# Attention with v stationary: p*v for two heads on column halves, probabilities scaled before the product, three parts summed in PSUM

## The chip, the cores and the metric

The kernel runs on one core of one Trainium2 chip. The metric is device time in microseconds (us), the median over repeated executions. One execution was also recorded by the profiler; its rows are the ones shown here. TensorE is the matrix engine, VectorE (DVE), ScalarE (ACT) and GpSimd (POOL) work beside it, and SyncE issues the weight loads.

## The reference, cut to what matters

Three transformer blocks run one after the other on 512 tokens of width 1024. The first has an attention of 8 heads over 512 keys with a multiplicity bias (called b1 here), a memory attention of 4 heads over 256 keys (mem), and a convolution branch with a layer norm. The two that follow (layers 0 and 1 of the second block, "layers" below) each have a causal attention with a forget gate (fox, 8 heads), and an attention (nsa, 8 query heads, 2 key heads) whose output is a gated sum of three parts:

```python
p_s = softmax(where(valid_s, s, -inf)); o_s = einsum('bgrqk,bgqkd->bgrqd', p_s, vg)   # selected: sel
p_w = softmax(where(valid_w, s, -inf)); o_w = einsum('bgrqk,bgkd->bgrqd', p_w, vwin)  # window: win
p_c = softmax(where(valid_c, s, NEG_BIG)) * valid_c; o_c = einsum('bgrqn,bgnd->bgrqd', p_c, vc)
o_n = g[..., 0:1] * o_c + g[..., 1:2] * o_s + g[..., 2:3] * o_w
```

With 512 tokens, 8 blocks of 64 and 16 to be selected, every block is selected, and the window of 512 covers all keys, so sel and win are both plain causal attentions. o_c has 31 compressed keys.

## The kernel before, in words

Each engine has a program written out by hand; semaphores order them. Weights stream from memory in blocks of 128x1024 through a ring of three slots; POOL splits each block into a high and a low part (L372, L375), and `linear` (L406) does three matmuls per 128x128 chunk (L422 to L424), the third with the low part. A split of block b waits until TensorE is done with block b-3. After a tile, an engine takes the PSUM bank (`took`), and the next tile on that bank waits for that.

The attentions run in *units*: one head, one tile of 128 queries. Units come in pairs of heads that sit on the two row halves (partitions 0 to 63 and 64 to 127) of the q and k tiles. Block 1 has 32 b1 units of 512 keys, then 16 mem units of 256. A layer has 32 fox units, then 32 sel, then 32 win units; their rows have 128 keys times (query tile + 1), in the order of tiles 0, 2, 1, 3.

`attend` is one loop per engine over the unit index i, with stages that lag:

- TensorE (L506): q*k of units i and i+1 in every second step (L533), with the gate rows and causal masks of the layers added to the bank (L540, L541); the transposes of p of unit i-2 (L547); p*v of unit i-4 with the transposed p stationary and the 64 columns of v moving (L567). Then what fills the step: `between1` (layer norm over the convolution and transposes of outputs, in block 1), `compressed` (the attention on 31 keys, during fox), or, during sel and win, two of the eight chunks of a gate tile (six matmuls), all gate tiles on bank 3. After the loop come transposes of the outputs (`turn_out`).
- ScalarE (L865): tanh of a gate tile, copy of the transposed p (L880), exp with its row sum (L887).
- VectorE (L1227): first, every fourth unit, the gate tile off bank 3 (L1234); then the row minimum of the new pair (L1243 for b1, L1246 otherwise), one convolution tap (L1177), `compressed`, and for unit i-4 the reciprocal of the sum (L1257), for sel and win the product with the gate (L1260), and the scaling of the output into `o1`, `oa` or `on` (L1265, L1271).

At the end of a layer's attention the outputs `oa` and `on` are transposed (L503), copied (L921) and split (L1277) for the output projection (`mix`). In block 1 `o1` goes the same way (L607, L646).

```python
mm = nc.tensor.matmul(ps[6 + j % 2][:, 0:HD], pT[:, j % 3, c * P:(c + 1) * P], v_,
                      start=c == 0, stop=c == n - 1)
...
if c0 == 0:
    if bank in last_on_bank:
        pe.wait_ge(*took(last_on_bank[bank]))
```

Of the kernel before, what the change touches and what calls it, by code (L numbers as in the profile page):

```python
# [17 lines left out]
P = 128  # L18
S = 512
D = 1024  # L20
DC = D // P
# [22 lines left out]
IN1_TAPS = {5: 4, 8: 3, 11: 3, 14: 3, 17: 5, 18: 3, 19: 5, 20: 3, 21: 4}  # L44
# [22 lines left out]
def build(nc, xT, memT, positions, wstream, params, fconst, bconst, lncount, trig2, out):  # L67
# [4 lines left out]
    with ctx:  # L72
# [26 lines left out]
        lnr = at("lnr", [S], f32, T + 12 * KIB)  # L99
        lni = at("lni", [S], f32, T + 14 * KIB)  # L100
# [5 lines left out]
        o1 = at("o1", [TT, 768], f32, R + 51 * KIB)  # L106
        lnc = at("lnc", [TT, S], f32, R + 67 * KIB)
        srow = at("srow", [2, S], f32, R + 75 * KIB)
# [19 lines left out]
        vsw = at("vsw", [2, TT, P], f32, R + 48 * KIB)  # L128
        kc = at("kc", [2, NCMP], f32, R + 52 * KIB)
        vbd = at("vbd", [2, 256], f32, R + 52 * KIB + 512)  # L130
        hidc = at("hidc", [2, 2, 62], f32, R + 54 * KIB + 512)
        gates = at("gates", [TT, 24], f32, R + 55 * KIB + 512)
        c3 = at("c3", [S], bf16, R + 56 * KIB)
        lf = at("lf", [TT, 8], f32, R + 57 * KIB)
        fgs = at("fgs", [S], f32, R + 57 * KIB + 128)
        z32 = at("z32", [3, TT, 32], f32, R + 59 * KIB + 256)
        s8 = at("s8", [5, TT, 8], f32, R + 60 * KIB + 896)
        oa = at("oa", [TT, 512], f32, R + 66 * KIB)
        on = at("on", [TT, 512], f32, R + 74 * KIB)
# [6 lines left out]
        ya_hi = at("ya_hi", [4, S], f32r, R + 32 * KIB)  # L146
        ya_lo = at("ya_lo", [4, S], f32r, R + 40 * KIB)
        yn_hi = at("yn_hi", [4, S], f32r, R + 48 * KIB)
        yn_lo = at("yn_lo", [4, S], f32r, R + 56 * KIB)
        mt = at("mt", [2, S], f32, R + 74 * KIB)  # L150
# [10 lines left out]
        prow = at("prow", [3, S], f32, T)  # L161
        pT = at("pT", [3, S], f32, T + 6 * KIB)
        crow = at("crow", [256], f32, T + 12 * KIB)
        cprob = at("cprob", [8, 32], f32, T + 13 * KIB)
        cprobT = at("cprobT", [256], f32, T + 14 * KIB)
# [23 lines left out]
        def pcol(name, i=0, n=1):  # L189
# [25 lines left out]
        scored, row_min, row_exp, p_turned, p_kept, pv_done, o_kept = (  # L215
            sem(n) for n in ("scored", "row_min", "row_exp", "p_turned", "p_kept", "pv_done", "o_kept"))
        conv_taps, ln_sum, ln_centred, ln_sq, ln_rt, ln_full, ln_hi, ln_lo = (
            sem(n) for n in ("conv_taps", "ln_sum", "ln_centred", "ln_sq", "ln_rt", "ln_full", "ln_hi", "ln_lo"))
        o_turned, o_hi, o_lo = sem("o_turned"), sem("o_hi"), sem("o_lo")
# [7 lines left out]
        c_scored, c_shift, c_exp, c_prob, c_turned, c_kept, c_pv, c_o = (  # L227
            sem(n) for n in ("c_scored", "c_shift", "c_exp", "c_prob", "c_turned", "c_kept", "c_pv", "c_o"))
# [82 lines left out]
        UN = [(k, p + 4 * r, t) for k in ("sel", "win") for p in range(4) for t in T_ORDER for r in range(2)]  # L311
# [12 lines left out]
        def turn_bank(u1, c):  # L324

            return (u1 + c) % 3 if c < 3 else c

        LN_AT, TURN_AT = 33, (38, 40, 42, 44)
        LIN_OF = {FIRST["fox", l]: l for l in range(LAYERS)}
# [36 lines left out]
        def _(pool):  # L366
# [16 lines left out]
            for b0, b1 in RUNS:  # L383
# [3 lines left out]
                for b in range(b0 + (b1 - b0) // RING * RING, b1):  # L387
                    split(b % RING, b // RING + 1, b)
                if b1 < NBLOCKS:
# [13 lines left out]
        def _(pe):  # L403
# [96 lines left out]
            def turn_out(src, bank):  # L500

                for t in range(TT):
                    mm = nc.tensor.transpose(ps[bank][:, t * P:(t + 1) * P], src[:, t, :], ident)  # L503
                mm.then_inc(o_turned, 1)

            def attend(u0, u1, gates_from=None, gate_tiles=()):  # L506

                for i in range(u0, u1 + 4):
                    if i < u1 and (i - u0) % 2 == 0:
                        kind, w = units[i][0], width(i)
                        plain = kind in ("b1", "mem")
                        if units[i] == ("mem", 0, 0):
                            pe.wait_ge(qk_final, len(QK))
                        for u in (i, i + 1):
# [11 lines left out]
                            if u - u0 < 3 and gates_from is not None:  # L529
                                pe.wait_ge(*took(last_on_bank[u % 3]))  # L530
                            if u - u0 >= 3:
                                pe.wait_ge(row_min if units[u - 3][0] == "b1" else row_exp, u - 2)
                            mm = nc.tensor.matmul(ps[u % 3][:, 0:w], q_, k_, start=True, stop=plain)  # L533
                            if plain:
                                mm.then_inc(scored, 1)
                        for u in () if plain else (i, i + 1):
                            _, h, t = units[u][:3]
                            bank = ps[u % 3]
                            if kind == "fox":
                                nc.tensor.matmul(bank[:, 0:w], headsel[0:96, h, :], c3[0:96, 0:w], start=False, stop=False)  # L540
                            nc.tensor.matmul(bank[:, t * P:w], identb, causal, start=False, stop=True).then_inc(scored, 1)  # L541
                    j = i - 2
                    if u0 <= j < u1:

                        pe.wait_ge(row_exp, j + 1)
# [1200 lines left out]
```

## Time and profile before

| | before |
|---|---|
| median of 3 runs | 2360.43 us (2360.38 to 2363.29) |
| profiled execution, its own time | 2360.79 us |
| its span | 2359.0 us |
| TensorE busy / weight loads | 2303.8 us (98%) / 1869.4 us |
| VectorE, ScalarE, POOL busy | 1194.3 (51%), 596.6 (25%), 1486.9 us (63%) |
| granted TensorE clock, mean | 0.991 |
| first q*k to first output matmul, block 1 | 166.5 to 261.2 us |
| layer 0: fox, sel and win, tail to the mix | 833.6, 885.3, 1058.2, 1067.2 us |

Busy time of TensorE ends where a model of its pipeline ends, so its matmuls overlap in the rows: what one costs in a row of many is the distance between starts. An fp32 matmul counts as two instructions, one per pass; a transpose is one. "x8 in 1.00 us" is eight instructions merged into one row, from the first start to the last end.

### The profile page before, as it was taken

What the parts mean: (1) busy time and instruction counts of PE and PEld (TensorE: products, weight loads), DVE (VectorE), ACT (ScalarE), POOL (GpSimd) and SP (SyncE); (2) the same over time, 40 slices, a digit from 0 to 9 for tenths busy, and PEclk for the clock granted to TensorE, in tenths of its full rate; (3) what the DMA queues carried; (4) which work ended last, traced back from release to release, by engine and by line L of the source; (5) the groups of instructions that cost most, each with busy time, mean ns of one, the idle gap of its engine ahead of it and who ended that gap; (6) DMA issues with size and microseconds to landing.
All of it is one profiled execution on the core that took longest, in us unless ns stands there. A gap on an engine that the chain in (4) does not pass through costs nothing.

```text
span 2359.0 us, 30891 instructions
## 1 busy us (share of the span) xinstructions
PE 2303.8 (98%) x11620; PEld 1869.4 (79%) x11620; DVE 1194.3 (51%) x1902; ACT 596.6 (25%) x1333; POOL 1486.9 (63%) x677
## 2 busy tenths in 40 slices
PE   6999899999999999999999999999999999999998
PEld 5877788888887877777888888877777788888886
DVE  6467667774344165667641143451556677420422
ACT  4236422221021154441220021111443422200210
POOL 5650377788876513346788788754424367887884
PEclk9999999999999999999999999999999999999999
DMA  5220133333333311112233322233101122232332
GB/s 197 81 81 1 36 96 93 97 98 101 105 98 107 101 34 37 54 45 81 88 100 98 98 93 96 98 95 102 63 28 50 50 70 91 95 95 96 99 99 71
DMA packets 53837, 195.87 MB, mean 83 GB/s; under 512 B 6096, under 2 KB 6096, under 8 KB 53456
## 3 DMA queue, kind: packets, MB, share of 16 engines
q1 hardware_dynamic: 51408, 187.72, 24.7%
q10 hardware_dynamic: 2304, 6.37, 0.7%
q8 instruction: 92, 1.51, 0.3%
q14 instruction: 33, 0.27, 0.0%
HBM read 191.97 MB, written 2.10 MB: 82 GB/s over the span
## 4 chain that ended last, share of the span: by engine, by line
PE 92%; DVE 4%; DMA 1%; issue 1%; ACT 1%; POOL 1%; SPq 0%; DVEq 0%; POOLq 0%
PE bank L422 25%; PE bank L424 25%; PE bank L423 24%; PE bank L567 5%; PE bank L533 4%; PE bank L547 3%; PE bank L498 1%; PE bank L541 1%; PE bank L438 1%; DMA w_raw<-wstream 1%; PE bank L459 1%; PE bank L540 1%; DVE vbd L1461 0%; PE bank L489 0%; POOL w_lo L375 0%
## 5 line engine op out<-in xcount | busy, mean ns | idle before, releaser
L372 POOL TENSOR_TENSOR w_hi<-w_raw,zero 128x1024 fp32r<-128x1024 f32 x336 | 643.3, 1915 | 819.5 <-PE bank L424 736.2
L375 POOL TENSOR_TENSOR w_lo<-w_raw,w_hi 128x1024 fp32r<-128x1024 f32 x336 | 845.2, 2515 | 26.4
L422 PE MATMUL bank<-hn_hi,w_hi 128*128 128x512 f32 x1632 | 659.9, 404 | 21.3 <-DVE hn_lo L1304 10.6
L424 PE MATMUL bank<-hn_hi,w_lo 128*128 128x512 f32 x1632 | 640.6, 392 | 0.0
L423 PE MATMUL bank<-hn_lo,w_hi 128*128 128x512 f32 x1632 | 639.2, 392 | 0.0
L422 PEld LDWEIGHTS bank<-hn_hi,w_hi 128*128 128x128 f32 x1632 | 309.2, 189 | 86.1 <-POOL w_lo L375 9.3
L424 PEld LDWEIGHTS bank<-hn_hi,w_lo 128*128 128x128 f32 x1632 | 308.3, 189 | 66.4
L423 PEld LDWEIGHTS bank<-hn_lo,w_hi 128*128 128x128 f32 x1632 | 309.4, 190 | 60.1 <-issue 2.2
L422 PE MATMUL bank<-hid_hi,w_hi 128*128 128x512 f32 x688 | 267.6, 389 | 0.0
L423 PE MATMUL bank<-hid_lo,w_hi 128*128 128x512 f32 x688 | 267.6, 389 | 0.0
L424 PE MATMUL bank<-hid_hi,w_lo 128*128 128x512 f32 x688 | 267.6, 389 | 0.0
L1283 DVE TENSOR_TENSOR x<-bank,x 128x512 f32<-128x512 f32 x64 | 44.3, 692 | 374.4 <-PE bank L424 374.4
L880 ACT ACTIVATE pT<-bank 128x256 f32<-128x256 f32 (+2 forms) x240 | 108.3, 452 | 205.2 <-PE bank L547 205.2
L424 PEld LDWEIGHTS bank<-hid_hi,w_lo 128*128 128x128 f32 x688 | 129.2, 188 | 26.9
L422 PEld LDWEIGHTS bank<-hid_hi,w_hi 128*128 128x128 f32 x688 | 129.2, 188 | 26.9
L423 PEld LDWEIGHTS bank<-hid_lo,w_hi 128*128 128x128 f32 x688 | 129.2, 188 | 26.5
L1100 ACT ACTIVATE sq<-tmp 128x512 f32<-128x512 f32 x64 | 40.4, 632 | 420.7 <-DVE tmp L1583 420.7
L1583 DVE SCALAR_TENSOR_TENSOR tmp<-bank,rs 128x512 f32<-128x512 f32 x64 | 44.1, 691 | 198.4 <-PE bank L424 185.1
L1246 DVE TENSOR_REDUCE cols<-bank 128x1 f32<-128x256 f32 (+1 forms) x208 | 91.2, 480 | 65.4 <-PE bank L541 58.8
L1587 DVE TENSOR_TENSOR hid_lo<-sq,hid_hi 128x512 fp32r<-128x512 f32 x64 | 119.1, 1866 | 1.5 <-ACT hid_hi L1102 1.5
L887 ACT ACTIVATE prow<-bank,cols 128x256 f32<-128x256 f32 (+1 forms) x208 | 108.1, 520 | 42.1 <-DVE cols L1246 38.7
L547 PE MATMUL bank<-fc,prow 128*128 128x128 f32 x640 | 111.3, 277 | 1.7 <-ACT prow L887 1.7
(292 smaller groups left out, 2853.6 us busy)
## 6 DMA issues: line engine op xcount, KB each, us to landing
w_raw<-wstream SPq DMA_DIRECT2D x352, 512.0 KB, 3.5
x<-xT SPq DMA_DIRECT2D x4, 512.0 KB, 7.8
out<-yout ACTq DMA_DIRECT2D x8, 256.0 KB, 2.2
mem_x<-memT SPq DMA_DIRECT2D x1, 1024.0 KB, 12.7
lnc<-lncount ACTq DMA_DIRECT2D x1, 1024.0 KB, 6.8
cs<-trig ACTq DMA_DIRECT2D x2, 512.0 KB, 3.7
par<-params ACTq DMA_DIRECT2D x1, 696.0 KB, 8.7
fc<-fconst ACTq DMA_DIRECT2D x1, 592.0 KB, 6.9
```

Source lines behind the costliest of these rows:

```text
L372: nc.gpsimd.tensor_tensor(w_hi[:, slot, :], w_raw[:, slot, :], zeros, ALU.add).then_inc(w_rounded, 1)
L375: nc.gpsimd.tensor_tensor(w_lo[:, slot, :], w_raw[:, slot, :], w_hi[:, slot, :].bitcast(f32), ALU.subtract).then_inc(w_split, 1)
L422: nc.tensor.matmul(ps[bank][:, 0:cols_], wh, a_h, start=c == 0, stop=False)
L423: nc.tensor.matmul(ps[bank][:, 0:cols_], wh, a_l, start=False, stop=False)
L424: mm = nc.tensor.matmul(ps[bank][:, 0:cols_], wl, a_h, start=False, stop=c == chunks - 1)
L533: mm = nc.tensor.matmul(ps[u % 3][:, 0:w], q_, k_, start=True, stop=plain)
L547: mm = nc.tensor.transpose(ps[4 + j % 2 * 1][:, c * P:(c + 1) * P], prow[:, j % 3, c * P:(c + 1) * P], ident)
L567: mm = nc.tensor.matmul(ps[6 + j % 2][:, 0:HD], pT[:, j % 3, c * P:(c + 1) * P], v_, start=c == 0, stop=c == n - 1)
L880: A(pT[:, j % 3, 0:w], ps[4 + j % 2][:, 0:w], ACT.Copy).then_inc(p_kept, 1)
L887: A(prow[:, i % 3, 0:w], src, ACT.Exp, scale=-1.0, bias=cols[:, 0, i % 64:i % 64 + 1], accum_out=cols[:, 1, i % 64:i % 64 + 1]).then_inc(r ...
L1246: V.tensor_reduce(mn, ps[u % 3][:, 0:w], AX.X, ALU.min).then_inc(row_min, 1)
L1587: V.tensor_tensor(hid_lo[:, i - 1, :], sq[:, (n - 1) % 2, :], hid_hi[:, i - 1, :].bitcast(f32), ALU.subtract).then_inc(ff_lo, 1)
```

## The change

- p*v: the 64 columns of v are stationary and the transposed p (128 columns) moves; the two heads of a pair write partitions 0 to 63 and 64 to 127 of bank 6. The output is thereby already transposed; `o1`, `oa`, `on` and all transposes of outputs go. ScalarE and VectorE copy and split it straight into the operands of the next projection.
- The rows of p are scaled before they are transposed: by POOL times 1/sum in b1, mem and fox (after POOL has split the three weight blocks that the ring holds), by VectorE times gate/sum in sel and win, where POOL splits the gate weights. The compressed probabilities are scaled likewise.
- sel and win units alternate. sel, win and the compressed part of a pair are summed in PSUM, in one group of matmuls.
- The loop advances by pairs; transposes lag by 4 units, p*v by 6; score banks are four (0, 1, 2, 7), `prow` and `pT` have four slots. In sel and win the causal matmuls come after p*v, and four chunks of a gate tile (twelve matmuls) fill a pair.
- VectorE takes the gate tile after the row minima of the new pair. In mem it copies every second transposed row.
- Block 1: the layer norm works out its inverse root as four columns and spreads it by matmuls; both halves of the convolution accumulate in bank 3; nine more taps run before the attention.

```diff
+            def scale_rows(u0, u1):
+                for u in range(u0, u1):
+                    w, r = width(u), cols[:, 2, u % 64:u % 64 + 1]
+                    pool.wait_ge(row_ri, SCALER[u][1])
+                    nc.gpsimd.tensor_tensor(prow[:, u % 4, 0:w], prow[:, u % 4, 0:w],
+                                            bass.AP(r.tensor, r.offset, [r.ap[0], [0, w]]), ALU.mult).then_inc(p_scaled, 1)
...
-        UN = [(k, p + 4 * r, t) for k in ("sel", "win") for p in range(4) for t in T_ORDER for r in range(2)]
+        UN = [(k, p + 4 * r, t) for p in range(4) for t in T_ORDER for k in ("sel", "win") for r in range(2)]
...
@@ TensorE, attend
-                for i in range(u0, u1 + 4):
...
+                for i in range(u0, u1 + 6, 2):
+                    j = i - 4
+                    if u0 <= j < u1:
+                        for u in (j, j + 1):
+                            pe.wait_ge(*SCALER[u])
+                            if u - 2 >= u0:
+                                pe.wait_ge(*KEPT[u - 2])
...
+                    j = i - 6
                     if j >= u0:
...
+                        if kind != "win" and j:
+                            pe.wait_ge(o_lo, outputs_before(j))
                         for c in range(n):
+                            for u in (j, j + 1):
+                                h = units[u][1]
+                                rows = slice(HD * (u - j), HD * (u - j) + HD)
...
+                                mm = nc.tensor.matmul(ps[6][rows, 0:P], v_, pT[:, u % 4, c * P:(c + 1) * P],
+                                                      start=c == 0 and kind != "win",
+                                                      stop=c == n - 1 and kind not in ("sel", "win"))
+                        if kind == "win":
+                            for u in (j, j + 1):
+                                h, g = units[u][1] % 4, u - j
+                                mm = nc.tensor.matmul(ps[6][HD * g:HD * g + HD, 0:P], vbd[:, g, h * HD:(h + 1) * HD],
+                                                      cprobT[:, t, g * P:(g + 1) * P], start=False, stop=True)
...
+                    if i < u1 and units[i][0] in ("sel", "win"):
+                        for u in (i, i + 1):
+                            t = units[u][2]
+                            nc.tensor.matmul(s_bank(u)[:, t * P:width(u)], identb, causal, start=False,
+                                             stop=True).then_inc(scored, 1)
+                    for n in (i, i + 1):
...
+                        elif n < u1:
+                            c = 2 * (n - gates_from)
...
+                            linear(gate_tiles[c // 8], hn_hi, hn_lo, S, DC, part=(c % 8, c % 8 + 2))
@@ ScalarE, attend: per pair: compressed and tanh, two copies, exp, the output copy, exp
+                    j = i - 6
+                    if j >= u0 and units[j][0] != "sel":
+                        act.wait_ge(pv_done, outputs_before(j) + 1)
+                        A(output(j)[0], ps[6][:, 0:P], ACT.Copy).then_inc(o_hi, 1)
@@ VectorE, attend
+                    j = i - 2
+                    if u0 <= j < u1:
+                        for u in (j, j + 1):
...
+                            if kind in ("sel", "win"):
+                                link(V.reciprocal(r, cols[:, 1, k:k + 1]))
+                                a_ = 3 * h + (1 if kind == "sel" else 2)
+                                link(V.tensor_tensor(g, r, gates[:, t, a_:a_ + 1], ALU.mult))
+                                V.tensor_scalar(prow[:, u % 4, 0:w], prow[:, u % 4, 0:w], g, None, ALU.mult).then_inc(p_gated, 1)
+                            else:
+                                V.reciprocal(r, cols[:, 1, k:k + 1]).then_inc(row_ri, 1)
+                    if i < u1:
+                        for u in (i, i + 1):
...
+                            dve.wait_ge(scored, u + 1)
...
+                    for n in (i, i + 1):
...
+                        if 0 <= g < len(gate_tiles) and (n - gates_from) % 4 == 0:
...
+                            dve.wait_ge(blocks_done, filled(gate_tiles[g]))
+                            V.tensor_tensor(sg[:, g, :], ps[3][:, :], rs[:, :], ALU.mult).then_inc(dve_took, 1)
+                    j = i - 6
+                    if j >= u0 and units[j][0] != "sel":
+                        dve.wait_ge(o_hi, outputs_before(j) + 1)
+                        hi, lo = output(j)
+                        V.tensor_tensor(lo, ps[6][:, 0:P], hi.bitcast(f32), ALU.subtract).then_inc(o_lo, 1)
```

## Rows read from the trace of the kernel before

**Rows 1.** The page: the chain that ended last, by engine.
```profile
PE 92%; DVE 4%; DMA 1%; issue 1%; ACT 1%; POOL 1%; SPq 0%; DVEq 0%; POOLq 0%
```
**Rows 2.** Busy time by stretch: PE, PEld, DVE, ACT, POOL, then PE clock, DMA share, GB/s.
```profile
166.50:261.20 94.70, 88.39 (x609) 67.18 (x609) 73.58 (x216) 64.37 (x157) 1.05 (x1) 0.96 0.02 7
833.60:885.30 51.70, 51.42 (x398) 40.50 (x398) 33.09 (x112) 30.14 (x101) 3.38 (x2) 1.00 0.07 21
885.30:1058.20 172.90, 172.90 (x1057) 132.04 (x1057) 104.34 (x269) 70.54 (x209) 64.21 (x30) 1.00 0.14 46
```
**Rows 3.** Timeline of TensorE in b1: start, duration, line; one iteration.
```profile
183.25 1.13 PE L533 MATMUL bank<-k,q 64*128 64x512 f32 x4
...
184.81 1.00 PE L567 MATMUL bank<-v,pT 128*128 128x64 f32 x8
185.65 0.61 PE L547 MATMUL bank<-fc,prow 128*128 128x128 f32 x4
186.09 1.00 PE L567 MATMUL bank<-v,pT 128*128 128x64 f32 x8
187.03 1.13 PE L533 MATMUL bank<-k,q 64*128 64x512 f32 x4
```
**Rows 4.** Timeline of TensorE in sel: q*k and the start of six gate matmuls.
```profile
890.46 0.92 PE L533 MATMUL bank<-ksw,qb 64*128 64x384 f32 x4
...
892.36 0.48 PE L422 MATMUL bank<-hn_hi,w_hi 128*128 128x512 f32 x1
892.68 0.39 PE L423 MATMUL bank<-hn_lo,w_hi 128*128 128x512 f32 x1
892.91 0.39 PE L424 MATMUL bank<-hn_hi,w_lo 128*128 128x512 f32 x1
...
896.31 0.70 PE L533 MATMUL bank<-ksw,qb 64*128 64x256 f32 x4
```
**Rows 5.** Timeline of TensorE: a narrow stationary side; q*k of one head alone.
```profile
826.35 0.64 PE L776 MATMUL bank<-par,hidc 128*31 128x64 f32 x8
...
836.91 0.70 PE L533 MATMUL bank<-ka,qa 64*128 64x256 f32 x2
```
**Rows 6.** Timeline of sel/win, layer 0: row minima, a causal matmul, a gate tile taken.
```profile
885.96 0.49 DVE L1246 TENSOR_REDUCE cols<-bank 128x1 f32<-128x128 f32 x2 [0.23 <-PE bank L541]
...
1042.72 0.28 PE L541 MATMUL bank<-bc 128*128 128x128 bf16 x2
...
1042.98 1.02 DVE L1246 TENSOR_REDUCE cols<-bank 128x1 f32<-128x384 f32 x2 [1.48 <-PE bank L541]
...
1047.84 0.69 DVE L1234 TENSOR_TENSOR sg<-bank,rs 128x512 f32<-128x512 f32 x1 [1.09 <-PE bank L424]
...
1053.79 1.29 DVE L1246 TENSOR_REDUCE cols<-bank 128x1 f32<-128x512 f32 x2 [1.21 <-PE bank L541]
```
**Rows 7.** Timeline at the start of layer 0's mix.
```profile
1064.64 2.48 DVE L1277 TENSOR_TENSOR ya_lo<-bank,ya_hi 128x512 fp32r<-128x512 f32 x4
...
1067.17 0.50 PE L422 MATMUL bank<-ya_hi,w_hi 128*128 128x512 f32 x1 [0.42 <-DVE ya_lo L1277]
```
**Rows 8.** POOL's split, and by line: counts, duration ns min/median/max.
```profile
834.71 2.35 POOL L375 TENSOR_TENSOR w_lo<-w_raw,w_hi 128x1024 fp32r<-128x1024 f32 x1
...
L1260 DVE TENSOR_TENSOR cols<-cols,gates x128: 159/230/2051, 898.1 to 1902.5; 128x1 f32<-128x1 f32 x128
...
L1323 DVE TENSOR_SCALAR angle<-angle x1: 428/428/428, 31.7 to 31.7; 128x512 f32<-128x512 f32 x1
```
**Rows 9.** Timeline of ScalarE in b1.
```profile
185.50 0.71 ACT L887 ACTIVATE prow<-srow,cols 128x512 f32<-128x512 f32 x1
...
186.29 0.60 ACT L880 ACTIVATE pT<-bank 128x512 f32<-128x512 f32 x1
```
**Rows 10.** Timeline of the mem units: the layer norm's reciprocal and TensorE after it.
```profile
238.60 3.35 DVE L1190 RECIPROCAL lni<-lnr 128x512 f32<-128x512 f32 x1 [2.10 <-ACT lnr L897]
...
243.85 1.11 PE L567 MATMUL bank<-vm,pT 128*128 128x64 f32 x4 [2.64 <-DVE o L1271]
```

More of the change, by code:

```diff
@@ L322, in width, with s_bank, output, outputs_before @@
             return S if kind == "b1" else NMEM if kind == "mem" else P * (t + 1)
-        def turn_bank(u1, c):
-            return (u1 + c) % 3 if c < 3 else c
-        LN_AT, TURN_AT = 33, (38, 40, 42, 44)
+        LN_AT = 30
         LIN_OF = {FIRST["fox", l]: l for l in range(LAYERS)}
+        KEPT, SCALER, OUTPUT = {}, {}, {}
+        for u in range(NU):
+            sem_, by_dve = (p_kept_dve, True) if units[u][0] == "mem" and u % 2 else (p_kept, False)
+            KEPT[u] = (sem_, 1 + sum(1 for v in KEPT.values() if v[0] is sem_))
+            sem_ = p_gated if units[u][0] in ("sel", "win") else p_scaled
+            SCALER[u] = (sem_, 1 + sum(1 for v in SCALER.values() if v[0] is sem_))
+            if u % 2 == 0:
+                OUTPUT[u] = len(OUTPUT) - sum(1 for v in OUTPUT if units[v][0] == "sel")
+        def s_bank(u):
+            return ps[(0, 1, 2, 7)[u % 4]]
+        def output(u):
+            kind, h, t = units[u][:3]
+            cols_ = slice(t * P, (t + 1) * P)
+            if kind in ("b1", "mem"):
+                c = h // 2 + (6 if kind == "mem" else 0)
+                return mix_hi[:, c, cols_], mix_lo[:, c, cols_]
+            if kind == "fox":
+                return ya_hi[:, h // 2, cols_], ya_lo[:, h // 2, cols_]
+            return yn_hi[:, h % 4, cols_], yn_lo[:, h % 4, cols_]
+        def outputs_before(u):
+            return sum(1 for v in range(0, u, 2) if units[v][0] != "sel")
         RUNS = [(RING, B_L + TURNS), (B_L + TURNS + 24, B_L + LAYER_BLOCKS + TURNS),
@@ L536, in attend @@
[L536 to L545, printed above, removed]
-                        for c in range(width(j) // P):
-                            mm = nc.tensor.transpose(ps[4 + j % 2 * 1][:, c * P:(c + 1) * P],
-                                                     prow[:, j % 3, c * P:(c + 1) * P], ident)
-                        mm.then_inc(p_turned, 1)
@@ L550, in attend @@
-                    j = i - 4
+                            gated_ = kind in ("sel", "win")
+                            mm = nc.tensor.matmul(s_bank(u)[:, 0:w], q_, k_, start=kind != "fox", stop=not gated_)
+                            if not gated_:
+                                mm.then_inc(scored, 1)
+                    j = i - 6
                     if j >= u0:
-                        kind, h, t = units[j][:3]
+                        kind, _, t = units[j][:3]
                         n = width(j) // P
-                        if i >= u1:
-                            pe.wait_ge(p_kept, j + 1)
-                        if j >= 2 and j - 2 >= u0:
-                            pe.wait_ge(o_kept, j - 1)
+                        for u in (j, j + 1):
+                            pe.wait_ge(*KEPT[u])
+                        if kind != "win" and j:
+                            pe.wait_ge(o_lo, outputs_before(j))
@@ L1176, in conv_tap @@
                     dve.wait_ge(conv_taps, n)
-                    ins = V.scalar_tensor_tensor(out=conv_acc[:, 0, :] if c == 0 and k == CONV_K - 1 else run, in0=src,
+                    ins = V.scalar_tensor_tensor(out=conv_acc[:, c, :] if k == CONV_K - 1 else run, in0=src,
                                                  scalar=w, in1=run, op0=ALU.mult, op1=ALU.add)
```

379 lines of the change are left out of this document (162 added, 217 removed).

## The prediction

> **What bounds the kernel now.** I read the page first, then busy time by stretch, then TensorE's order of work inside each attention, then its helpers. The page gives TensorE 92% of the chain that ended last [rows 1]. By stretch, TensorE is busy for all 172.9 us of layer 0's sel/win stage, for 51.42 of 51.70 us of its fox stage and for 88.39 of 94.70 us of block 1's attention [rows 2]. So the question is always what TensorE issues and what it waits for. A b1 iteration (two heads) is transposes, p*v, transposes, p*v, q*k, without a hole: 183.25 to 187.03 is 3.78 us [rows 3]. The eight p*v matmuls take 184.81 to 185.65 = 0.84 us: 0.105 us each, though they stream only 64 columns (a transpose takes 0.44/4 = 0.11 [rows 3]; I use 0.107 for both). p is the stationary side there, and loading its 128 columns sets the pace. In sel/win TensorE fills each unit with six gate matmuls [rows 4].
>
> **The change, part by part** (minus is faster; both layers counted).
>
> 1. *p\*v.* There are 320 chunks of 128 keys counted by pairs of heads (16x4 in b1, 8x2 in mem, 2x120 in the layers: 12 pairs of heads, whose four query tiles have 1 to 4). Each costs 4 x 0.107 = 0.427 us now. Afterwards each head has two passes that stream 128 columns. The price of such a pass: q*k of 384 columns shows 0.92 us where one of 256 shows 0.70 [rows 4]: 0.22 for 128 columns more over two passes, so 0.11 a pass. Whether two heads on column halves run at once no row shows; on row halves they do: one head alone takes 0.70 us and two heads of that width take 0.70 as well [rows 4, 5]. A stationary side below 128 columns with all rows in use keeps its loads hidden (eight passes of 64 columns in 0.64 us, a last one being 0.22, so 0.06 each) [rows 5]. Bounds per chunk: 0.21 (full overlap) and 0.43 (none), with 0.32 if about half the price of a load, 0.05, lies bare in front of each pass (an estimate: 64 of the 128 columns that take 0.107). I take 0.22, by the row halves: 320 x 0.207 = -66.2. The Trainium skill (TensorE: Matmul & The Clock Gate, Part 3) measures three column tiles at 2.38 times one tile's rate; at that efficiency two tiles would give 1.59 and the sum would be some 15 us higher. No run shows it yet.
>
> 2. *Switches between array shapes.* Going into q*k costs 0.10: 186.09 to 187.03 is 0.94 where the same p*v took 0.84 [rows 3]. The new order has three shapes per pair instead of two: 120 pairs x 0.10 = +12. The Trainium skill (TensorEngine Tiling, Key Properties) says that a change of tiling mode drains the engine; by that rule, which speaks against this change, the trace agrees.
>
> 3. *Output transposes* go: 88 of 0.107 (16+8 in block 1, 32 in each layer) = -9.4. The compressed product moves from a step of its own into the win units with about the same streaming: 0. Gate matmuls now come in twelves: 64 restarts less at 0.32 - 0.23 = 0.09 (892.36 to 892.68 against 892.68 to 892.91 [rows 4]) = -5.8.
>
> 4. *A new wait in sel/win.* All gate tiles share bank 3, and TensorE may start tile g+1 only when VectorE has taken tile g. Before, VectorE did this first in its iteration (L1234). Now it first reduces the two rows of the new pair, and these wait for the causal matmuls, which TensorE now issues last before the gate matmuls. So at each of the 15 later tiles of a layer TensorE stands idle: the reduction starts 0.26 us after the first causal matmul (1042.72 to 1042.98); the two take 0.49 us at the narrowest tile and 1.29 at the widest, in even steps, so 0.89 in the mean; L1234 takes 0.69, some 0.66 in a row; then 0.05 to the engine (1067.12 to 1067.17) [rows 6, 7]. Without the wait it would go on some 0.21 after that causal matmul (an estimate: one more, and the restart). 0.26 + 0.89 + 0.66 + 0.05 - 0.21 = 1.65; 30 x 1.65 = +49.5. Behind the waiting gate matmuls are queued the next pair's transposes and q*k, so nothing fills the hole. Bounds: 1.3 (narrow rows) to 2.1.
>
> 5. *Fox.* Scaling goes exp, reciprocal, POOL, and TensorE transposes two pairs later. POOL is still splitting a weight block until 837.06 when the layer's first rows are ready [rows 8]; TensorE then waits for the first rows (1.1), again for the second pair, whose exps come behind the compressed part on both helpers (1.4 and 0.7), and for the third (0.5): about 3.7 us, estimates from following the first iterations in program order. Once per four pairs ScalarE waits, ahead of its copies, for compressed transposes that TensorE issues at the end of the same iteration; its copy of them (some 0.4) and one row copy (some 0.5) delay the next transposes, and the exps behind them the pair after (0.3): 1.25 each time, six more times. 7.4 + 7.5 = +15. Bounds: 0 if ScalarE's and VectorE's slack in fox covers it (30 and 33 of 52 us busy [rows 2]), 30 if every second pair slips like this.
>
> 6. *The port.* POOL splits a block in two operations, the second of 2.35 us [rows 8], right after each gate tile. L1260, on a 128x1 column, takes 0.16 us free and up to 2.05 beside it [rows 8]. The row scaling (0.43 for 128x512 free [rows 8]) can wait likewise. Only after the widest pair does it land there ahead of the reductions: 8 times, about half of them at 2.1: +8. Bounds 0 and +63 (all 30). The Trainium skill (SBUF — State Buffer, glossary) calls this an exclusive lock that blocks the loser for a whole instruction; the row agrees.
>
> 7. *Block 1.* By 1 and 2 a b1 pair needs 3.78 - 4x0.207 + 0.10 = 3.05 us of TensorE. ScalarE needs, start to start, 2 x 0.79 (exp with its sum) + 2 x 0.60 (copy) + 0.25 (new output copy of 128x128, an estimate below half of that 128x512 copy) = 3.0 [rows 9], and the loop of reduction (0.6), exp, output copy, exp and reciprocal (0.2), with 0.3 for the signals, makes 0.6 + 0.79 + 0.25 + 0.79 + 0.2 + 0.3 = 2.93. Three things near 3.0 in engines that work in order give 3.3: +4. A mem pair has half the width: TensorE 1.7, the loop some 2.3 by the same terms: 8 x 0.6 = +4.8. Estimates for the ends: first pair and the two taps ahead of it +3.5; layer norm output after the loop +2; its matmuls +0.6; tail +1. The 128x512 reciprocal (3.35 us) with TensorE's 2.64 us wait, and the matmuls behind it at about double time (1.11 for four, where eight take 1.00 in rows 3), go: -7.5 [rows 10]. TensorE's half speed there shows in the granted clock of 0.96 over the stretch [rows 2]. Together +8.4. The nine taps moved ahead of the attention (0.75 us each) fall into VectorE's waits between the q and k tiles but for the last two, which stand in the 3.5. Each p*v now also waits until VectorE has split the output before it, since bank 6 is alone: some 2.5 to 3.2 us after q*k, against 3.05; that is part of the 3.3.
>
> Sum: -66.2 + 12 - 9.4 - 5.8 + 49.5 + 15 + 8 + 8.4 = +11.5 us. The profiled execution took 2360.8 us (span 2359.0), 0.4 above the median of 2360.43, so I forecast 2372. The idle 0.42 us at a layer's mix [rows 7] stays about as it is. Costed at nothing: reciprocals and POOL's row work in steady b1 (1.2 us per row at most, half of 2.35 for half the length [rows 8]: two rows fit a 3.3 us iteration), and VectorE's 64 row scalings per layer in sel/win, where it is busy for 104 of 173 us [rows 2]; if that cover goes, some 0.1 and 0.4 us per pair. The DMAs are the same in number and size.
>
> **The rivals.**
> - *TensorE stays the bound in block 1 and fox.* The helpers keep up, which removes item 5 and 4 + 4.8 of item 7. For it: ScalarE was busy only 30 of 52 us in fox [rows 2]. Against: the loops are worked out within 0.1 us of TensorE's need. It decides at a b1 pair under 3.1 us. 2372 - 24 = 2348: faster. Chance 0.22.
> - *Loads stay exposed in the column tiles,* half a load in front of each pass: 0.32 a chunk, 320 x 0.1 = +32: 2404. Chance 0.13.
> - *The column halves run one after the other,* so that the change does not do what it says: +66: 2438. Only the row halves speak against it. 0.07.
> - *The port decides:* scaling falls into POOL's split at every gate tile: +55: 2427. The row of L1260 shows such waits now, yet the operations then stand elsewhere in the order. 0.06.
> - *Only some of item 5 and 7 is real:* 2356 to 2365, no change that can be told. 0.12.
>
> **How the numbers follow.** My forecast (a slowdown between 2365 and 2395, the wait on bank 3 outweighing what p*v saves in sel/win) has 0.40. A measurement of this kernel tells 0.2%, 4.7 us, from no change. Faster: the first rival, 0.22. Same: 0.12. Slower: 0.40 + 0.13 + 0.07 + 0.06 = 0.66. The range runs from the first rival to just past exposed loads, 2345 to 2410; it leaves out the serial halves and the port. The slowdown's own range is 2365 to 2395.
>
> **What would show it.** Right: in sel/win TensorE waits some 1.6 us, fifteen times per layer, before L422 for VectorE's gate product, and twelve gate matmuls follow at 0.23; the new p*v lines take about 0.22 us per chunk for both heads; the sel/win stage of 172.9 us grows by some 15 us although p*v shrinks; block 1's attention falls from 94.7 to about 87. Wrong in 1: a p*v line at 0.4 us per chunk. Wrong in 4: gate matmuls right behind the causal ones. Wrong in 5 and 7: b1 pairs at 3.05 us and no idle before the row transposes. I am wrong on the sign if the sel/win stage comes out shorter than 172.9 us.

## The result, and the profile after

| | before | after |
|---|---|---|
| median of 4 runs each | 2360.6 us | 2389.2 us (2386.0 to 2390.2) |
| ratio, 95% interval | | 1.0116 (1.0103 to 1.0128) |
| profiled execution, its span | 2360.8, 2359.0 us | 2390.2, 2388.0 us |
| block 1's attention | 94.7 us | 85.2 us |
| linear work up to layer 0's fox | 572.4 | 577.8 |
| fox, layers 0 and 1 | 51.7, 51.8 | 51.3, 55.2 |
| sel, win and tail, layers 0 and 1 | 181.9, 181.9 | 197.0, 196.8 |

The change made the kernel 28.6 us slower, 1.2%; I had forecast +11.5. The stages are those of [rows 2], from the first q\*k of one to that of the next (after the change fox starts with the gate rows, which now come 0.3 us ahead of q\*k); sel and win are taken with the tail behind them, since after the change no tail stands apart. What is not listed differs by 0.4 us at most.

The chain by engine, after (it answers to [rows 1]). TensorE gives up 4 points, VectorE takes 3 of them.
```profile
PE 88%; DVE 7%; POOL 2%; ACT 1%; DMA 1%; issue 1%; SPq 0%; DVEq 0%; POOLq 0%
```
Busy time by stretch after, columns as in [rows 2]: block 1, fox 0, sel/win/tail 0, fox 1.
```profile
166.70:251.90 85.20, 74.77 (x604) 46.46 (x604) 58.41 (x188) 59.69 (x165) 43.20 (x49) 0.96 0.03 8
829.70:881.00 51.30, 43.43 (x368) 28.42 (x368) 26.93 (x99) 30.09 (x109) 23.73 (x32) 1.00 0.07 21
881.00:1078.00 197.00, 172.39 (x1166) 125.86 (x1165) 85.06 (x294) 73.43 (x235) 70.62 (x34) 0.99 0.13 41
1682.60:1737.80 55.20, 47.31 (x368) 30.49 (x368) 27.73 (x101) 30.38 (x109) 24.76 (x32) 0.91 0.06 20
```
In none of the three attentions is TensorE busy all the time any more: it stands still for 24.6 of 197 us in sel and win and for 7.9 of 51.3 in fox. What it waits for, over the whole program (total us, times, longest):
```profile
PE bank L462 <- DVE sg L1279: 46.5, 30, 1.9
...
PE bank L550 <- POOL prow L418: 9.5, 10, 4.6
PE bank L604 <- DVE ya_lo L1284: 8.5, 13, 0.8
...
PE bank L550 <- ACT pT L908: 7.0, 10, 0.7
```
The first row is the wait on bank 3: L462 is the first matmul of a gate tile, L1279 the product with which VectorE takes the tile before (L1234 before). TensorE's timeline around one such place:
```profile
931.29 0.68 DVE L1279 TENSOR_TENSOR sg<-bank,rs 128x512 f32<-128x512 f32 x1
...
932.02 0.50 PE L462 MATMUL bank<-hn_hi,w_hi 128*128 128x512 f32 x1 [1.12 <-DVE sg L1279]
...
934.89 1.03 PE L550 MATMUL bank<-fc,prow 128*128 128x128 f32 x8
935.85 0.49 PE L581 MATMUL bank<-ksw,qb 64*128 64x128 f32 x4
936.27 1.09 PE L604 MATMUL bank<-pT,vsw 128*64 128x128 f32 x16
937.30 0.28 PE L617 MATMUL bank<-bc 128*128 128x128 bf16 x2
937.40 0.48 PE L462 MATMUL bank<-hn_hi,w_hi 128*128 128x512 f32 x1
```
From there on everything follows without a hole. The "128*64" of the p\*v row (L604) is the column half; 16 instructions, four chunks of both heads, take 936.27 to 937.30.

### The profile page after: what moved, and what is told of

Read it like the earlier page. It is cut to its first block, busy times and chain, and to the rows that moved or that the text cites. A ratio compares the mean times of both kernels' runs of the same rounds, so it can differ in the third digit from the quotient of the medians.

```text
span 2388.0 us, 31243 instructions
## 1 busy us (share of the span) xinstructions
PE 2265.3 (95%) x11648; PEld 1803.3 (76%) x11648; DVE 1109.9 (46%) x1864; ACT 588.7 (25%) x1391; POOL 1574.3 (66%) x789
## 4 chain that ended last, share of the span: by engine, by line
PE 88%; DVE 7%; POOL 2%; ACT 1%; DMA 1%; issue 1%; SPq 0%; DVEq 0%; POOLq 0%
PE bank L462 25%; PE bank L464 24%; PE bank L463 24%; PE bank L581 3%; PE bank L604 3%; PE bank L550 3%; DVE cols L1266 2%; PE bank L538 1%; DVE sg L1279 1%; POOL prow L418 1%; PE bank L478 1%; DMA w_raw<-wstream 1%; PE bank L499 1%; PE bank L617 1%; DVE bank L1190 0%
## 5 line engine op out<-in xcount | busy, mean ns | idle before, releaser
L398 POOL TENSOR_TENSOR w_lo<-w_raw,w_hi 128x1024 fp32r<-128x1024 f32 x336 | 845.1, 2515 | 26.4
L462 PE MATMUL bank<-hn_hi,w_hi 128*128 128x512 f32 x1632 | 657.4, 403 | 67.9 <-DVE sg L1279 46.5
L462 PEld LDWEIGHTS bank<-hn_hi,w_hi 128*128 128x128 f32 x1632 | 309.8, 190 | 141.1 <-DVE sg L1279 51.7
L462 PE MATMUL bank<-hid_hi,w_hi 128*128 128x512 f32 x688 | 267.6, 389 | 0.0
L1266 DVE TENSOR_REDUCE cols<-bank 128x1 f32<-128x256 f32 (+3 forms) x208 | 91.0, 479 | 157.6 <-PE bank L617 133.8
L418 POOL TENSOR_TENSOR prow<-prow,cols 128x512 f32<-128x512 f32 (+3 forms) x112 | 87.1, 799 | 100.0 <-DVE cols L1256 100.0
L462 PEld LDWEIGHTS bank<-hid_hi,w_hi 128*128 128x128 f32 x688 | 129.1, 188 | 26.9
L890 ACT ACTIVATE prow<-bank,cols 128x256 f32<-128x256 f32 (+3 forms) x208 | 109.6, 529 | 111.4 <-DVE cols L1266 111.4
L550 PE MATMUL bank<-fc,prow 128*128 128x128 f32 x640 | 97.8, 283 | 17.6 <-POOL prow L418 9.5
```

The lines of the kernel that those rows point to most:

```text
L398: nc.gpsimd.tensor_tensor(w_lo[:, slot, :], w_raw[:, slot, :], w_hi[:, slot, :].bitcast(f32), ALU.subtract).then_inc(w_split, 1)
L418: nc.gpsimd.tensor_tensor(prow[:, u % 4, 0:w], prow[:, u % 4, 0:w], bass.AP(r.tensor, r.offset, [r.ap[0], [0, w]]), ALU.mult).then_inc(p_s ...
L462: nc.tensor.matmul(ps[bank][:, 0:cols_], wh, a_h, start=c == 0, stop=False)
L550: mm = nc.tensor.transpose(ps[4 + u % 2][:, c * P:(c + 1) * P], prow[:, u % 4, c * P:(c + 1) * P], ident)
L890: A(prow[:, u % 4, 0:w], src, ACT.Exp, scale=-1.0, bias=cols[:, 0, u % 64:u % 64 + 1], accum_out=cols[:, 1, u % 64:u % 64 + 1]).then_inc(r ...
L1266: V.tensor_reduce(mn, s_bank(u)[:, 0:w], AX.X, ALU.min).then_inc(row_min, 1)
```

## The experiments

All times are medians beside runs of the kernel before on the same chip (2360.9 to 2362.2 there). Stages are from one profiled execution each.

### Is the bank wait the cost? (two orders on VectorE)

**First of all.** VectorE takes the gate tile at the start of its step.
```diff
                 for i in range(u0, u1 + 6, 2):
+                    g = -1 if gates_from is None else (i - gates_from) // 4 - 1
+                    if 0 <= g < len(gate_tiles) and (i - gates_from) % 4 == 0:
...
+                        dve.wait_ge(blocks_done, filled(gate_tiles[g]))
+                        V.tensor_tensor(sg[:, g, :], ps[3][:, :], rs[:, :], ALU.mult).then_inc(dve_took, 1)
                     j = i - 4
```


> The changed kernel with one move: VectorE takes the gate tile off bank 3 at the start of its step, ahead of the scalings and row minima of the new pair. Theory (the bank wait): the 30 waits before the gate matmuls go (23.2 us of idle per layer in the trace, some 26 with the restart of the pipeline after each), about -52 us, to 2337 us, and the sel/win stage with its tail falls from 197 to about 171 us. Rival (the work on VectorE only moves): the reductions and with them the exps come 0.7 us later in every second pair and TensorE waits for those instead, so only half or less comes back: 2362 us or more. If the wait was not what costs, 2389.

Measured: 2357.6 us (0.9981 of before, 0.9972 to 0.9990), sel/win/tail 181.9 us. The 30 waits on bank 3 are gone, but only 32 of 52 us came back. In their place TensorE has 38 waits for VectorE that it did not have before, 16.3 us (p\*v for the split output, the transposes for the scaled rows):
```profile
PE bank L604 <- DVE yn_lo L1284: 8.8, 28, 0.5
PE bank L550 <- DVE prow L1262: 7.5, 10, 3.1
```
VectorE shows why; by line in layer 0's sel and win (count, busy us, mean ns), first after, then here:
```profile
L1254 DVE TENSOR_SCALAR prow<-prow,cols 128x128 f32<-128x128 f32 (+3 forms) x64 | 24.8, 387 | 2.3
...
L1253 DVE TENSOR_TENSOR cols<-cols,gates 128x1 f32<-128x1 f32 x64 | 10.2, 159 | 2.2
```
```profile
L1262 DVE TENSOR_SCALAR prow<-prow,cols 128x128 f32<-128x128 f32 (+3 forms) x64 | 60.1, 940 | 2.3
...
L1261 DVE TENSOR_TENSOR cols<-cols,gates 128x1 f32<-128x1 f32 x64 | 26.0, 407 | 2.2
```
The same 64 scalings take 60.1 us in place of 24.8. One place in the timeline:
```profile
933.36 0.69 DVE L1243 TENSOR_TENSOR sg<-bank,rs 128x512 f32<-128x512 f32 x1 [2.40 <-PE bank L464]
933.97 0.15 DVE L1259 RECIPROCAL cols<-cols 128x1 f32<-128x1 f32 x1
934.16 1.16 DVE L1261 TENSOR_TENSOR cols<-cols,gates 128x1 f32<-128x1 f32 x1
935.35 2.50 DVE L1262 TENSOR_SCALAR prow<-prow,cols 128x128 f32<-128x128 f32 x1
```
```profile
933.41 1.89 POOL L395 TENSOR_TENSOR w_hi<-w_raw,zero 128x1024 fp32r<-128x1024 f32 x1 [6.62 <-PE bank L464]
935.38 2.39 POOL L398 TENSOR_TENSOR w_lo<-w_raw,w_hi 128x1024 fp32r<-128x1024 f32 x1
```
VectorE waits for the gate tile's last matmul, and so does POOL, which then splits the next weight block. The scalings queued behind the gate tile fall into that split: the 128x1 product ends with the first operation, the 128x128 scaling, 0.29 us elsewhere, with the second. The operation that reads PSUM (0.69; it began 0.05 us ahead of the split) and the reciprocal of one column (0.15) are not held. The Trainium skill (SBUF — State Buffer, glossary) has the loser of the shared ports block fully for the winner's whole instruction; the rows of the product and the scaling agree. The order alone makes the scalings late too, since they now stand behind VectorE's wait for the gate tile; no run here parts the two.

**Between scalings and minima.** The same lines, behind the scalings of pair i - 2 and ahead of the minima of pair i.

> The changed kernel with VectorE's gate tile taken between the row scalings of the pair before and the row minima of the new pair. With the gate tile first of all, the 30 bank waits went but only 32 us came back, because the row scalings then ran into POOL's split (operations of 0.29 us took 2.5) and a wait for the split output appeared. Theory (order against POOL's split): the scalings are again done before TensorE finishes the gate tile, so no collision and no bank wait: -52 us less some 5 for waits on the split output, about 2342 us, below the kernel before. Rival (the split output of bank 6 is late whatever the order, 28 waits of 0.3 and more): 2350 us. Rival (collisions happen in this place too): 2357 us.

Measured: 2333.1 us (0.9878 of before, 0.9863 to 0.9893), lower than expected. Sel and win in layer 0, columns as above:
```profile
878.66:1047.58 168.92, 167.54 (x1166) 124.12 (x1165) 91.03 (x294) 75.25 (x235) 71.15 (x34) 1.00 0.15 48
```
The stage falls by 28.1 us per layer, 1.87 us for each of 15 waits. The profile calls only 1.55 us of each idle (46.5/30), because its idle time counts from the modelled end of the two causal matmuls, 0.28 us after their start, where the gate matmuls follow after 0.10 when nothing is waited for: that is 0.18 more. Most of the rest is clock. The granted clock was 0.99 over the stage after the change and 1.00 here; in the copy-late run below, where the waits are all there and the clock was 1.00, the stage took 195.3 us in layer 0 and 195.5 in layer 1. So some 26.4 of the 28.1 us are the waits (1.76 each) and 1.7 the clock. Twice 28.1 is 56.2 us, within 0.1 of what the kernel gained (2389.2 to 2333.1). One line's place on VectorE turns the change from 1.2% slower to 1.2% faster.

### What makes the wait: whose order?

**Causal matmuls early**, right behind q\*k as before, VectorE's order as changed.
```diff
+                    if i < u1 and units[i][0] in ("sel", "win"):
+                        for u in (i, i + 1):
+                            t = units[u][2]
+                            nc.tensor.matmul(s_bank(u)[:, t * P:width(u)], identb, causal, start=False,
+                                             stop=True).then_inc(scored, 1)
                     j = i - 6
                     if j >= u0:
```


> The changed kernel with the causal matmuls of sel and win put back right behind q*k, ahead of p*v; VectorE's order as changed. Theory (the wait is made of causal, row minima, gate tile taken, in that order): the minima start one p*v earlier, about 1.0 us at the pairs that wait (2.5 chunks x 0.22 + 0.15, and 0.32 for the compressed product), so the 30 waits shrink from about 1.55 to 0.6 us each, -28 us; one switch of array shape more per pair, 64 x 0.1 = +6: about 2367 us. Rival (VectorE's order alone makes the wait): no change or +6, 2389 to 2396 us.

Measured: 2362.0 us, sel/win/tail 183.4 us. The wait shrank to
```profile
PE bank L462 <- DVE sg L1279: 19.3, 30, 0.9
```
27.2 us less where 28 was worked out, and the time fell by the same 27.2; the 6 us for one more switch do not show in it.

**The kernel before with this one part of the change:** its lines at L1234 moved behind the row minima.

> The kernel before with one part of the change alone: VectorE takes the gate tile after the row minima of the new pair instead of ahead of them. Theory (the order on VectorE makes the wait, and TensorE's causal matmuls issued last lengthen it): here the causal matmuls come ahead of transposes and p*v, some 0.87 us before the gate matmuls, so the wait is 0.26 + 0.89 + 0.66 + 0.05 - 0.87 = 1.0 us, thirty times: +30 us, 2391 us. Rival (it takes both orders together): the wait is hidden, 2360 to 2366 us.

Measured: 2384.8 us, 1.0099 of before (1.0082 to 1.0116): +23.0 of the 30 expected. Its wait:
```profile
PE bank L422 <- DVE sg L1246: 18.2, 30, 0.9
```
So the order on VectorE alone makes 0.6 us of idle time thirty times, and TensorE's causal matmuls issued last make it 1.55.

### Do the column halves run at once?

```diff
-                        for c in range(n):
-                            for u in (j, j + 1):
+                        for u in (j, j + 1):
+                            for c in range(n):
```


> The changed kernel with the two loops of p*v exchanged: all chunks of the first head on the lower column half, then all of the second on the upper one; same instructions, same values. Theory (two heads run at once because neighbouring instructions stand on different column halves): a chunk of both heads goes from 0.22 back to about 0.43 us, up to 320 x 0.21 = +67 us, less what the waits in block 1 and fox cover: 2430 to 2456 us, p*v groups of 16 at about 1.8 us instead of 1.03. Rival (the saving comes from the narrow stationary side alone, not from running at once): 2389 us, groups unchanged.

Measured: 2417.8 us (two executions), +28.5, against 41 to 67 expected. The group of 16 in b1 took 1.51 us start to start, against 1.03 after:
```profile
185.88 1.58 PE L604 MATMUL bank<-pT,v 128*64 128x128 f32 x16
187.39 1.09 PE L550 MATMUL bank<-fc,prow 128*128 128x128 f32 x8
```
Shorter groups show where that comes from, here with three chunks of both heads and with two:
```profile
885.35 1.12 PE L604 MATMUL bank<-pT,va 128*64 128x128 f32 x12 [0.79 <-DVE ya_lo L1284]
886.40 0.28 PE L617 MATMUL bank<-bc 128*128 128x128 bf16 x2
...
890.72 0.67 PE L604 MATMUL bank<-pT,va 128*64 128x128 f32 x8
891.32 0.29 PE L617 MATMUL bank<-bc 128*128 128x128 bf16 x2
```
With 1, 2, 3 and 4 chunks the halves in turn take 0.37, 0.60, 1.05 and 1.51 us, alternating 0.37, 0.59, 0.81 and 1.02. Up to two chunks the order makes no difference. From there each further chunk costs 0.45 us in turn, 0.11 for each of its four passes, the price that the prediction gave to passes one after another, and 0.22 alternating. So alternating matters in the long groups, and there the two halves run fully at once, which excludes that the saving comes from the narrow stationary side alone. The factor, 0.45 to 0.22, is 2.1. The Trainium skill (TensorE: Matmul & The Clock Gate, Part 3) has 2.38 for three column tiles; the 1.59 that I estimated from it for two is too low for these groups. What the whole kernel lost fits the groups: 24 sets of the layers at 0.01 + 0.24 + 0.48 us make 17.5, block 1 grew by 3.6, and the rest, some 7 us, goes with the granted clock, 0.97 over sel and win in place of 0.99.

### Fox and block 1

**ScalarE's copy of the compressed probabilities one pair later** (the copy-late run).
```diff
-                if step == 5:
+                if step == 7:
                     act.wait_ge(c_turned, done + 1)
```


> The changed kernel with ScalarE's copy of the compressed probabilities moved one pair later in its program (fox only). Theory (fox's bubbles come from ScalarE standing still for the compressed transposes ahead of its row copies, 7.6 us in four waits per layer): TensorE's waits for the row copies (2.9 us per layer) and for the output splits (3.7) mostly go, -8 to -12 us over both layers: about 2379 us. Rival (they come from the path over POOL or from two pairs of lag being too short): the waits stay, 2387 to 2391 us.

Measured: 2381.7 us (2374.2 to 2385.9, wider than the others). The profiled execution was the fastest, 2374.2, so its stages tell more than the median gained. Fox took 48.9 and 48.9 us, against 51.3 and 55.2; the clock was 1.00 in both, against 1.00 and 0.91, and 2.4 us in each layer are what the bubbles were worth. ScalarE's waits in layer 0's fox, after:
```profile
ACT cprobT L938 <- PE bank L673: 7.6, 4, 2.1
```
The row is gone in the experiment, and TensorE's waits for row copies in fox with it (2.9 us in each layer). Its waits for the output split stayed (3.7 us in each layer): there the theory fell.

**Rows of fox scaled by VectorE.**
```diff
+                            elif kind == "fox":
+                                link(V.reciprocal(r, cols[:, 1, k:k + 1]))
+                                V.tensor_scalar(prow[:, u % 4, 0:w], prow[:, u % 4, 0:w], r, None,
+                                                ALU.mult).then_inc(p_gated, 1)
```


> The changed kernel with the rows of fox scaled by VectorE (reciprocal and product on one engine) instead of POOL; block 1 stays with POOL. Theory (ScalarE's order, not POOL, makes fox's bubbles): only the waits for POOL's rows go, 2.6 us over both layers, and half of those are for the exp anyway: 2386 us. Rival (the path exp, VectorE, POOL, TensorE is what makes fox late): the output waits go as well, -8 us or more: 2381 us or less.

Measured: 2393.3 us, slower by 4: the path over POOL was not what holds fox (54.0 and 54.9 us). TensorE now waited 1.3 us for `cprob` in each layer, since the compressed part queues behind the scalings, and the clock fell in layer 0's fox too (0.94 over the stretch).

**Six taps later** in block 1.
```diff
-IN1_TAPS = {5: 4, 8: 4, 11: 4, 14: 4, 17: 6, 18: 4, 19: 6, 20: 4, 21: 4, 22: 2}
+IN1_TAPS = {5: 4, 8: 4, 11: 4, 14: 4, 17: 6, 18: 4, 19: 6, 20: 4}
...
-                if i < LN_AT and i % 3 != 2:
+                if i < LN_AT and i % 8 != 7:
```


> The changed kernel with the last six convolution taps ahead of the attention of block 1 moved into its loop (36 taps before it instead of 42, 26 of the 30 steps up to the layer norm hold one instead of 20). Theory (the six taps of 4.7 us hold back the first row minima, and TensorE, idle for 4.6 us, then runs at a granted clock of 0.72 over the first 12.4 us): 5 to 7 us come back at the start, 6 more pairs take 3.84 instead of 3.11 us, -4.4: about 2387 us. Rival (the first pairs are held by POOL and the two pairs of lag, not by the taps): nothing comes back and the later taps cost 4.4 us: 2393 us.

Measured: 2387.1 us; block 1's attention 85.5 us against 85.2. The fourth pair's q\*k came 11.2 us after the first, 12.4 with the taps ahead: 1.2 back, not 5 to 7, and the pairs with two taps took it away again. So the stage gained 1.2 us and lost 1.5, where 5 to 7 and 4.4 were expected: the 2387 us of the theory came out by luck, and for the first pairs the rival was nearer.

**Combinations.** The gate tile between, the copy late and fox on VectorE:

> Three edits on the changed kernel at once: the gate tile taken between scalings and minima, the compressed copy one pair later, the rows of fox scaled by VectorE. Theory (three separate stalls, which add up): that of the first alone, about 2342, less 7.5 (the second alone measured 2381.7 against 2389.2) and less 3: 2331 us, 1.2% below the kernel before. Rival (the stalls hide behind each other): within 3 us of the first alone.

Measured 2326.5 us. The first two alone:

> Two edits on the changed kernel: the gate tile taken between scalings and minima, and the compressed copy one pair later; fox rows scaled by POOL as changed. Theory (the two stalls are in different stages, and VectorE's scaling in fox brought nothing): 2333.1 - 7.5 = 2325.6 us, at or just below the three edits together (2326.5). Rival (VectorE's scaling does help once ScalarE no longer stalls): 2328 us or more.

Measured 2326.5 us (0.9850 of before, 0.9833 to 0.9866): the same, so VectorE in fox brings nothing, and I was wrong to leave room for 3 us. The split of bank 6 ahead of taps and compressed work:

> The same two edits, and VectorE splits the output of bank 6 ahead of its taps and its compressed work instead of behind them. Theory (what is left in fox and block 1 is p*v waiting for the split before it: 9.1 and 2.4 us in 18 waits): half to most of it goes, -6 us: 2320 us. Rival (the split waits for ScalarE's copy between two exps, and the compressed work or the taps behind it come late in their turn): 2326 to 2332 us.

Measured 2329.4 us: p\*v's waits for the split fell from 11.4 to 6.7 us, and the waits for POOL's rows rose from 10.5 to 16.1. The rival held: VectorE's turn for the reciprocals comes late instead.

### The compressed product

```diff
-                        if kind == "win":
-                            for u in (j, j + 1):
-                                h, g = units[u][1] % 4, u - j
-                                mm = nc.tensor.matmul(ps[6][HD * g:HD * g + HD, 0:P], vbd[:, g, h * HD:(h + 1) * HD],
-                                                      cprobT[:, t, g * P:(g + 1) * P], start=False, stop=True)
```


> The two edits of before (gate tile between, copy late) and the product with the compressed values left out of the win units, so the compressed part is missing from the output. It prices the term that the prediction put at 0 against the old form, which took 3.7 us of TensorE per layer. Theory (four instructions of 0.08 us in each of 32 groups of products: 2.6 us per 32, 5.2 us per layer, all on TensorE's path since nothing waits there): 2326.5 - 10.4 = 2316 us. Rival (no more than the old form's 3.7 us per layer is to be had): 2319 us. Rival (a wait behind it takes its place): above 2322 us.

Measured: 2317.8 us, 8.7 less than with it; sel and win 165.4 instead of 168.9 us, 3.5 us per layer. Four of these instructions take 0.32 us in the trace, but 0.10 of it is the switch out of the column halves, which p\*v then pays. So the first rival was the right one, and 0 against the old 3.7 was right.

## Why the prediction was right in direction and too small

The sign, the place and the mechanism held; the forecast for sel and win was +9 us per layer with the tail, and 15 came. By its steps:

**Items 1 and 2, p\*v with its switch, are the step that failed in size: -54.2 forecast, some 17 less came.** I priced every group of p\*v at 0.107 us an instruction, read from full b1 groups [rows 3]. Groups of the kernel before in sel and win, with 1, 3 and 4 chunks of one head, each with the row behind it:
```profile
940.66 0.33 PE L567 MATMUL bank<-vsw,pT 128*128 128x64 f32 x2
940.80 0.47 PE L422 MATMUL bank<-hn_hi,w_hi 128*128 128x512 f32 x1
...
945.72 0.78 PE L567 MATMUL bank<-vsw,pT 128*128 128x64 f32 x6
946.30 0.47 PE L422 MATMUL bank<-hn_hi,w_hi 128*128 128x512 f32 x1
...
934.81 1.00 PE L567 MATMUL bank<-vsw,pT 128*128 128x64 f32 x8
935.62 0.48 PE L422 MATMUL bank<-hn_hi,w_hi 128*128 128x512 f32 x1
```
With 1 to 4 chunks they take 0.14, 0.36, 0.58 and 0.81 us: 0.22 per chunk, less 0.08 for each group. After, for both heads, in order of time 3, 2, 4 and 1 chunks:
```profile
882.30 0.88 PE L604 MATMUL bank<-pT,va 128*64 128x128 f32 x12 [0.80 <-DVE ya_lo L1284]
883.11 0.29 PE L617 MATMUL bank<-bc 128*128 128x128 bf16 x2
...
887.41 0.66 PE L604 MATMUL bank<-pT,va 128*64 128x128 f32 x8
888.00 0.29 PE L617 MATMUL bank<-bc 128*128 128x128 bf16 x2
...
892.10 1.09 PE L604 MATMUL bank<-pT,va 128*64 128x128 f32 x16
893.12 0.29 PE L617 MATMUL bank<-bc 128*128 128x128 bf16 x2
...
899.08 0.44 PE L604 MATMUL bank<-pT,vsw 128*64 128x128 f32 x4
899.45 0.28 PE L617 MATMUL bank<-bc 128*128 128x128 bf16 x2
```
0.81, 0.59, 1.02 and 0.37 us: 0.217 per chunk, as forecast, plus 0.15 per group where I had 0.10. A pair therefore saves -0.09, 0.13, 0.35 and 0.60 us with 1 to 4 chunks, 0.99 for the four query tiles of a head pair; I had 10 x 0.207 - 0.40 = 1.67. With one chunk the new form is slower. 24 such sets make 24 x 0.68 = 16.3 us, b1's full groups (2 x 0.84 - 1.03 = 0.65 against 0.73) 1.2 more.

**Item 3.** Output transposes: 32 in a layer took some 4.1 us by starts, 3.4 forecast. Gate restarts as forecast. The compressed product: right, above; it moved 3.5 us per layer into sel and win and 3.7 out of fox.

**Item 4, the wait on bank 3:** +49.5 forecast, 56.2 measured by taking it away, within its bounds (1.87 each, 1.3 to 2.1). From the causal to the gate matmul 1.83 us pass in the mean, where 1.86 was worked out; so the sum of parts held. What was too small: without the wait TensorE goes on after 0.10 us, not after the estimated 0.21 (3 us in all), and 3.4 us of lower clock stand in the 56.2, for which the forecast had no term.

**Item 5, fox:** +15 forecast. Fox grew by 3.0 us in both layers together. By the groups above p\*v saved 4 x 0.99 = 4.0 and the moved product 3.7 per layer, so the bubbles cost 3.0 + 15.4 = 18 us; nearly 4 of it are layer 1's clock. ScalarE's wait, 7.6 us in four times, was the one described.

**Item 6, the port:** +8 forecast, nothing came: the scaling in sel and win never took over 0.49 us after the change. It was priced in the wrong order; there VectorE's late gate tile keeps the scalings out of POOL's split. The collision is real once the gate tile stands first, and that place costs 24 us (2357.6 against 2333.1), the later start of the scalings included. That is the mechanism of the rival "the port decides", in a kernel that wasn't the one forecast.

**Item 7, block 1:** the attention shrank by 9.5 us where the terms gave 10.4 (80 chunks -16.6, 24 switches +2.4, 24 output transposes -2.6, item 7 without the layer norm's end +6.4). A pair without a second tap takes 3.1 us, with it 3.84, and the mean is the 3.3 of the forecast. The linear work behind it grew by 5.4 us, not 2: TensorE waits 2.1 us for the layer norm's last split, and its matmuls at 257 to 261 us then start 0.43 apart in place of 0.23, 1.6 us more; 1.7 us more go from 670 to 680 us, where the granted clock was 0.83. A term for the clock was missing.

By stage the misses are: block 1 +0.9, linear work +3.4, fox +1.4, sel and win +11.8 (p\*v +10.9, bank wait +6.7, port -8, the compressed product moved in +7.0, which fox gives back, outputs, causal matmuls and the wait at the mix about -4; these meet the 11.8 within a microsecond). Together 17.5, where the time missed by 17.1 us.

Of the rivals, the first (TensorE stays the bound in fox and block 1) is excluded by the idle time, exposed loads and serial halves by 0.217 us a chunk.

## What to carry to other kernels

Before an operation is moved within an in-order engine's program, list both what waits for it and what it will then run beside: here the same product cost 56 us behind the minima and 24 us ahead of the scalings, each against its place between them. Price short groups of matmuls from short groups: a form that wins by 0.6 us with four chunks loses with one, because it pays 0.15 us per group, where the old form's first chunk is cheap (0.14). From three chunks on, two narrow outputs gain from the column halves only if the instructions alternate between them.

## What the runs showed of the hardware that I had not expected

The granted clock fell in places that the holes alone do not explain. Layer 1's fox has the same work as layer 0's, and took 55.2 us against 51.3; its start by stretches, after:
```profile
1685.00:1690.00 5.00, 3.19 (x14) 1.46 (x14) 3.22 (x12) 1.64 (x5) 4.22 (x5) 0.76 0.35 109
1690.00:1695.00 5.00, 4.27 (x16) 2.48 (x16) 1.08 (x4) 2.59 (x9) 1.48 (x3) 0.50 0.01 2
1695.00:1700.00 5.00, 5.00 (x39) 3.12 (x36) 2.20 (x7) 3.08 (x12) 1.67 (x2) 0.71 0.00 0
```
After waits of 1.55 and 0.26 us (at 1687.4 and 1688.0) TensorE ran at half its clock (1.2 of 2.4 GHz) for some ten microseconds, while it was 85 to 100% busy. But the copy-late run has the same two waits at the same place, and the granted clock stayed 1.00:
```profile
1679.01 0.33 PE L550 MATMUL bank<-fc,prow 128*128 128x128 f32 x1 [1.59 <-POOL prow L418]
1679.55 0.33 PE L550 MATMUL bank<-fc,prow 128*128 128x128 f32 x1 [0.21 <-POOL prow L418]
```
And from 670 to 680 us after the change it fell with no wait at all (the same matmuls ran at 1.00 in the copy-late run):
```profile
670.00:680.00 10.00, 10.00 (x42) 8.19 (x41) 0.00 (x0) 0.60 (x1) 3.98 (x2) 0.83 0.15 49
```
What makes it fall is therefore not shown here. Nor is ScalarE's stall the reason in fox: the clock was down before the first wait for a row copy (1691.57), and in the run without the compressed product, where the copy is late, it fell behind the same two waits (1.57 and 0.24), and layer 1's fox took 49.9 us at 0.97. What these runs show is the price: of the 6.3 us between 55.2 and 48.9, 2.4 are the bubbles, as in layer 0, and 3.9 the clock; with the same code for fox, layer 1 took 53.3 to 55.2 us in five traces. Behind the waits at the start of block 1 the clock was 0.72 over the first 12.4 us.

Operations of VectorE differ in what POOL does to them. In the run with the gate tile first, a 128x1 product of two SBUF columns took up to 1.16 us where 0.16 is free, and a scaling of 128x512 up to 2.71 where 0.49 is free; reading a PSUM bank and a reciprocal took no longer than elsewhere.
